# RWKV scan and attention on one core: attention's pieces joined in every third step, the inversion's products on four 64x64 tiles

## Chip, cores and metric

One NeuronCore of a Trainium2 chip runs the whole program. The metric is the device time in microseconds of one execution; a run's number is that of the core, and the number compared is the median of the runs.

## The reference

Two transformer blocks on x of 1024 x 1024, float32. The change lies in the first one, which joins an attention branch (MLA) and an RWKV-7 branch in two directions. What matters of it:

```python
# attention, 8 heads, blocks of 128 queries, 1024 keys
s = einsum('bqhd,bkhd->bhqk', qn_b, k_nope) + einsum('bqhd,bkd->bhqk', qr_b, k_rope)
p = softmax(s * scale); o = einsum('bhqk,bkhd->bqhd', p, v)

# RWKV, 8 heads of 64, one scan forward and one backward over 1024 tokens
def step(state, inp):
    r_t, w_t, k_t, v_t, a_t, b_t = inp
    sa = einsum('bhvk,bhk->bhv', state, a_t)
    state = state * w_t[:, :, None, :] + sa[..., None] * b_t[:, :, None, :] + v_t[..., None] * k_t[:, :, None, :]
    return state, einsum('bhvk,bhk->bhv', state, r_t)
```

The kernel computes the scan in tiles of 128 tokens. Within a tile the feedback through a and b is a strictly triangular matrix N for each head, and the kernel needs the inverse of I - N. With a block D of N that is 16 wide the inverse is the product (I + D)(I + D^2)(I + D^4)(I + D^8); blocks of 16 are then put together to 32, 64 and 128.

## The kernel before

**Stages.** The program of each engine is a Python function that issues its instructions in order: PE (`tensor_program`), DVE (`vector_program`), ACT (`scalar_program`), POOL and SP (loads and stores). The stages follow each other: norm and projections, MLA, shift and preparation, then `scans` (536 to about 1340 us), after it the output projections, the FFN and the second block. The change touches `scans` alone.

**The order in `scans`.** Three generators run on each engine: scan 0 (forward), scan 1 (backward) and attention. `interleave` takes one step of each in turn, to the next `yield`, and does so in the same way on every engine; I call that a round. Scan 0 gets seven rounds' start. So each queue holds: a step of scan 0, a step of scan 1, a piece of attention, and so on. An engine takes its queue strictly in order, and waits on semaphores.

**A scan.** 8 tiles, each of 2 steps of transposes (T) and 2 x 13 steps for two halves of 4 heads (u = 0, 1): An (the products that give N), D2, D4, D8, X4 (the powers of D and the partial products X of the inverse), H1 and X5 (blocks of 16 to 32), H2 and T64 (to 64), V and Y, B (to 128), U (the solved feedback), O and S (output and state). `kinds` issues the masked products M behind D2 and D8. PE writes to PSUM, DVE and ACT bring the result to SBUF, where the next step reads it. In all that is 1 + 8 x 28 = 225 steps a scan, and 232 rounds.

**Products.** `diag` multiplies 4 heads x 2 halves of the partitions with tiles (0, 0) and (64, 64) of the array. `cross` sends two of the heads to the other half of the output's partitions, so that all four 64x64 tiles are used; as two rows of tiles must not write the same bank, its results lie in a pair of banks. D4 and D8 use `cross` already. One matmul of f32 gives two records in the trace.

**PSUM.** `take` gives out the 8 banks as a ring, in the order in which PE asks; with n=2 it starts at an even bank. PE waits there for those who read the bank's last content.

**Attention.** `att_steps` yields after each part: scores of head tile i (2 matmuls of 512 columns), the 8 transposes of the probabilities of i - 1, and after every second one the product with v. That is 1 + 64 + 64 + 32 = 161 pieces. DVE takes the maximum of the scores over 1024 keys and negates it (L1127 to L1135), ACT the exp (L1148), DVE the reciprocal of the sum and the scaling (L1120 to L1125, issued ahead of the next maximum), PE transposes (L358), ACT copies.

Lines that appear in the trace: L354 and L355 matmuls, L358 transposes, L361 ACT copies, L364 DVE and POOL elementwise operations, L375 DVE's maximum, L368 DVE's scaling and negation, L1148 exp, L1280 the store of a tile's output (scan 0 from EX, scan 1 from W). Scan 0 has its buffers in AR and EX, scan 1 in X, AR and W; HT and W1 belong to attention, CS holds constants.

## Time and profile before

| | us |
|---|---|
| median of 3 runs | 3516.8 (3514.44 to 3517.77) |
| profiled execution | 3505.72 |
| its span, first to last instruction | 3503.9 |
| scan stage with attention | 536 to 1181 |
| scan stage without | 1181 to about 1340 |

Over the whole span PE is busy 96%, DVE 49%, ACT 32%, POOL 9%, and the granted clock of PE is 0.991 of full speed on average, 0.95 to 1.00 in each 100 us. A busy PE is not a PE at its peak: a small matmul is drawn with a length of its own (0.22 us), whatever the distance to the next one. Idle time on an engine costs only where another one waits for it; the chain of waits says which.

### The profile page before, as it was taken

Reading aid. Unit: us, or ns where it says so; the run is one execution under the profiler, and the core shown is the slowest. Engines: PE = TensorE matmul, PEld = TensorE weight load, DVE = VectorE, ACT = ScalarE, POOL = GpSimd, SP = SyncE. Lnnn points to the kernel's source line nnn. Section 1 sums busy time; section 2 is a strip of 40 time slices with the busy share of each in tenths; the row PEclk is TensorE's granted clock in tenths of the full one; section 3 lists DMA queues with packets and bytes.
Section 4 is the critical chain, followed back from the end, with each engine's and each line's share of the span. In section 5 each row is a group of like instructions: output and inputs, shape, how many; then the busy total and the mean of one; then the engine's idle time right before and its main releaser. Section 6 shows DMA issues by size and latency. Waiting matters only on the chain.

```text
span 3503.9 us, 61009 instructions
## 1 busy us (share of the span) xinstructions
PE 3366.8 (96%) x27176; PEld 2664.1 (76%) x27176; DVE 1713.8 (49%) x2537; ACT 1112.9 (32%) x1799; POOL 322.6 (9%) x342
## 2 busy tenths in 40 slices
PE   8989998999999999999999999999999999999998
PEld 7678776777766785587888888787778788888877
DVE  5353564665666666654345434642554522352236
ACT  4323424444444331132124212432333311241124
POOL 1131241111111222000000000001000000000000
PEclk9999999999999999999999999999999999999999
DMA  3241253111210304421112211332003111121113
GB/s 143 67 149 43 72 189 107 59 38 41 71 59 31 113 21 151 144 84 49 49 48 96 73 48 48 108 104 98 25 31 120 63 51 49 61 96 55 49 67 107
DMA packets 89973, 269.84 MB, mean 77 GB/s; under 512 B 11552, under 2 KB 12080, under 8 KB 89712
## 3 DMA queue, kind: packets, MB, share of 16 engines
q1 hardware_dynamic: 78960, 230.29, 19.9%
q0 software_dynamic: 10752, 35.66, 3.0%
q8 instruction: 214, 3.51, 0.4%
q14 instruction: 47, 0.39, 0.0%
HBM read 219.77 MB, written 46.14 MB: 76 GB/s over the span
## 4 chain that ended last, share of the span: by engine, by line
PE 82%; DVE 10%; ACT 4%; issue 2%; DMA 1%; POOL 0%; SPq 0%; DVEq 0%; ACTq 0%; POOLq 0%
PE ps L355 77%; PE ps L354 3%; DVE SM L375 2%; PE ps L358 2%; DVE AR L364 2%; ACT HT L1148 1%; DVE X L364 1%; DVE HT L368 1%; DVE W L364 1%; ACT AR L361 1%; ACT WS L361 0%; DVE WS L364 0%; DVE EX L364 0%; ACT W L2074 0%; DMA qk_d<-AR 0%
## 5 line engine op out<-in xcount | busy, mean ns | idle before, releaser
L355 PE MATMUL ps<-HH,WS 128*128 128x512 f32 (+1 forms) x3232 | 997.6, 390 | 0.0
L355 PEld LDWEIGHTS ps<-HH,WS 128*128 128x128 f32 (+1 forms) x3232 | 605.2, 187 | 128.9
L355 PE MATMUL ps<-HL,WS 128*128 128x512 f32 x1616 | 637.7, 395 | 6.3 <-DVE HL L364 5.9
L364 DVE TENSOR_TENSOR WS<-W,WS 128x1024 fp32r<-128x1024 f32 x244 | 300.2, 1230 | 617.8 <-ACT WS L361 617.8
L361 ACT ACTIVATE WS<-W 128x1024 fp32r<-128x1024 f32 x244 | 256.6, 1051 | 843.4 <-PE ps L355 836.7
L355 PE MATMUL ps<-WS,SA 128*128 128x512 f32 x2112 | 486.7, 392 | 13.6 <-DVE SA L364 11.0
L355 PEld LDWEIGHTS ps<-WS,SA 128*128 128x128 f32 x2112 | 397.4, 189 | 101.1 <-issue 15.2
L355 PEld LDWEIGHTS ps<-HL,WS 128*128 128x128 f32 x1616 | 302.6, 187 | 71.6 <-issue 6.8
L355 PE MATMUL ps<-AR 64*64 64x64 f32 (+2 forms) x5440 | 200.1, 240 | 17.2 <-ACT AR L361 9.6
L364 DVE TENSOR_TENSOR SA<-HA,SA 128x512 fp32r<-128x512 f32 x176 | 121.5, 692 | 187.3 <-ACT SA L361 187.3
L355 PE MATMUL ps<-HL,HI 128*128 128x512 f32 (+1 forms) x512 | 208.1, 406 | 3.6 <-POOL WL L364 2.8
L355 PE MATMUL ps<-WS,HL 128*128 128x512 f32 x576 | 206.4, 392 | 0.8 <-DVE X L364 0.8
L355 PE MATMUL ps<-WS,HH 128*128 128x512 f32 x640 | 202.9, 393 | 3.6 <-issue 1.5
L355 PEld LDWEIGHTS ps<-AR 64*64 64x64 f32 (+1 forms) x5440 | 154.0, 135 | 68.0 <-issue 38.2
L355 PE MATMUL ps<-HH,HI 128*128 128x512 f32 (+1 forms) x512 | 205.3, 401 | 0.0
L355 PE MATMUL ps<-HH,WL 128*128 128x512 f32 (+1 forms) x512 | 204.7, 400 | 0.0
L361 ACT ACTIVATE SA<-HA 128x512 fp32r<-128x512 f32 x176 | 110.6, 631 | 282.2 <-PE ps L355 253.5
L355 PE MATMUL ps<-HT 96*128 96x512 f32 (+1 forms) x384 | 185.7, 617 | 0.3
L361 ACT ACTIVATE AR<-ps 128x512 f32<-128x512 f32 (+4 forms) x240 | 122.2, 522 | 120.4 <-PE ps L355 83.7
L364 DVE TENSOR_TENSOR HA<-HA,ps 128x512 f32<-128x512 f32 x88 | 60.4, 687 | 184.9 <-PE ps L355 184.1
L355 PEld LDWEIGHTS ps<-WS,HH 128*128 128x128 f32 x640 | 120.2, 188 | 29.7 <-issue 1.9
L364 DVE TENSOR_TENSOR AR<-ps,CS 128x512 f32<-128x512 f32 (+1 forms) x160 | 87.4, 580 | 111.9 <-ACT AR L361 45.3
(286 smaller groups left out, 4354.1 us busy)
## 6 DMA issues: line engine op xcount, KB each, us to landing
W<-in_w_fd SPq DMA_DIRECT2D x88, 512.0 KB, 3.4
AR<-rw_d SPq DMA_DIRECT2D x104, 256.0 KB, 4.1
W<-in_w_fg SPq DMA_DIRECT2D x44, 512.0 KB, 3.4
W<-in_w_fu SPq DMA_DIRECT2D x44, 512.0 KB, 3.4
W<-in_w_tok SPq DMA_DIRECT2D x24, 512.0 KB, 3.5
rw_d<-X POOLq DMA_DIRECT2D x40, 256.0 KB, 3.4
X<-in_x SPq DMA_DIRECT2D x16, 512.0 KB, 8.9
W<-in_w_g SPq DMA_DIRECT2D x16, 512.0 KB, 3.7
```

The source lines that it names most:

```text
L354: return pe.e.matmul(o, l, r, start=start, stop=stop, skip_group_check=True)
L355: return pe.e.matmul(o, l, r, start=start, stop=stop)
L358: return pe.e.transpose(o, i, ident)
L361: return e.e.activation(o, x, ACT.Copy)
L364: return e.e.tensor_tensor(o, x, y, op)
L368: return e.e.tensor_scalar(o, x, s1, None, o1)
L375: return e.e.tensor_reduce(o, x, AX.X, op)
L1148: ae.e.activation(APB[i % 2], ps[:, b:b + 2, :].rearrange("p a b -> p (a b)"), ACT.Exp, bias=sm(264 + i % 4, 1), scale=SCALE, accum_out=sm ...
```

## The change

- `att_steps` yields once for each head tile, after scores, transposes and (every second time) the product with v: 67 pieces. On ACT the transposes' copies come ahead of exp. `one_of_three` lets attention have every third round; in the seven first rounds it has every second one.
- D2, X4, H1 and X5 use `cross` and a pair of banks each. `cross` packs its results in 128 columns of each bank of the pair. An gets 4 matmuls more, which give a turned copy of two heads' blocks.
- Sums are made ahead of the product: with DI = D^k + I the product of DI and X is X + D^k X, so X is copied from PSUM by ACT and not added by DVE. DVE adds the unit matrix to the powers (`and_one`) after ACT's copy from the same banks. H1 and X5 do the same with G1 and X1.
- POOL's sum XA is made in two parts.
- The state product of O and O's products with v move behind the next `yield`, behind U.
- The table Z64 of zeros is no longer needed.

```diff
-        def att_steps(scores, transp, pv, load):
+        def att_steps(scores, transp, pv, load, copies_first=False):
             load(0)
             yield
             for i in range(66):
                 if i % 8 == 4 and i // 8 + 1 < 8:
                     load(i // 8 + 1)
-                if i < 64:
+                if i < 64 and not copies_first:
                     scores(i)
-                    yield
                 if 1 <= i <= 64:
                     transp(i - 1)
-                    yield
+                if i < 64 and copies_first:
+                    scores(i)
                 if i % 2 and i >= 3:
                     pv((i - 3) // 2)
-                    yield
+                yield
         def skip(*_):
...
-            return att_steps(scores, transp, pv, skip)
+            return att_steps(scores, transp, pv, skip, copies_first=True)
...
-            c.DX, c.XA = pair(2), heads(256)
-            c.plus = CS[:, len(CONST) * P:len(CONST) * P + P].rearrange("p (a n) -> p a n", a=2)
+            c.DI, c.XA, c.XB = [heads(256) for _ in range(3)]
+            c.eye = cst["I64"].unsqueeze(1).broadcast_to([P, 4, 64])
...
-                            x = mm(pe, ps[o, b + h // 2, 256 * m + c0:256 * m + c0 + 64], lhs[ROWS[z], h, :], rhs[ROWS[z], h, :],
+                            x = mm(pe, ps[o, b + h // 2, c0 + 64 * m:c0 + 64 * m + 64], lhs[ROWS[z], h, :], rhs[ROWS[z], h, :],
...
-                        for n in range(2):
-                            for js in ROWS:
+                        for n in range(2 + q):
+                            for z, js in enumerate(ROWS):
                                 for j, rows in enumerate(ROWS):
                                     at_, bt = c.ART[rows, p, 0, js], c.BT[rows, p, js]
-                                    x = mm(pe, ps[js, b + j, 128 * n + 64 * q:128 * n + 64 * q + 64], bt if n else at_,
+                                    c0 = 256 if n == 2 else 128 * n + 64 * q
+                                    x = mm(pe, ps[ROWS[1 - z] if n == 2 else js, b + j, c0:c0 + 64], bt if n else at_,
                                            at_ if n else bt, True, True)
                     x.then_inc(*pe.sig(PEs, "An", i, u))
                     yield
-                    b = take(pe, PEs, "D2", i, u)
+                    b = take(pe, PEs, "D2", i, u, n=2)
                     pe.wait_ge(*at(VEs, "D1", i, u, 1))
-                    diag(b, 0, c.D1[:, 1], c.D1[:, 0])
-                    diag(b, 256, c.D1[:, 0], c.D1[:, 1]).then_inc(*pe.sig(PEs, "D2", i, u))
+                    cross(b, 0, c.D1[:, 1], c.D1[:, 0])
+                    cross(b, 128, c.D1[:, 0], c.D1[:, 1]).then_inc(*pe.sig(PEs, "D2", i, u))
                     pe.wait_ge(*at(AEs, "T", i, 3))
                     kinds(i, u, 0)
                     yield
...
-                    cross(b, 64, c.DX[:, 0], c.XA).then_inc(*pe.sig(PEs, "D4", i, u))
+                    cross(b, 256, c.DI, c.XA).then_inc(*pe.sig(PEs, "D4", i, u))
                     yield
                     b = take(pe, PEs, "D8", i, u, n=2)
                     pe.wait_ge(*at(AEs, "D4", i, u))
                     cross(b, 0, c.D4[:, 1], c.D4[:, 0])
                     pe.wait_ge(*at(VEs, "D4", i, u))
-                    cross(b, 64, c.DX[:, 0], c.DX[:, 1]).then_inc(*pe.sig(PEs, "D8", i, u))
+                    cross(b, 128, c.DI, c.XB).then_inc(*pe.sig(PEs, "D8", i, u))
                     kinds(i, u, 1)
                     yield
-                    b = take(pe, PEs, "X4", i, u)
-                    pe.wait_ge(*at(AEs, "D8", i, u))
-                    diag(b, 0, c.DX[:, 0], c.DX[:, 1]).then_inc(*pe.sig(PEs, "X4", i, u))
-                    yield
-                    b = take(pe, PEs, "H1", i, u)
-                    pe.wait_ge(*at(VEs, "X4", i, u))
+                    b = take(pe, PEs, "X4", i, u, n=2)
+                    pe.wait_ge(*at(AEs, "X3", i, u))
+                    pe.wait_ge(*at(VEs, "D8", i, u))
+                    cross(b, 0, c.DI, c.XA).then_inc(*pe.sig(PEs, "X4", i, u))
+                    yield
+                    b = take(pe, PEs, "H1", i, u, n=2)
+                    pe.wait_ge(*at(AEs, "X4", i, u))
+                    cross(b, 0, c.X1[:, 1], c.eye)
                     pe.wait_ge(*at(GEs, "G2", i, u))
-                    for h in range(4):
-                        for js in ROWS:
-                            mm(pe, ps[js, b, 64 * h:64 * h + 64], c.X1[js, 1, h, :], ident[js, js], True, True)
-                    diag(b, 256, c.G1, c.X1[:, 1]).then_inc(*pe.sig(PEs, "H1", i, u))
-                    yield
-                    b = take(pe, PEs, "X5", i, u)
+                    cross(b, 128, c.G1, c.X1[:, 1]).then_inc(*pe.sig(PEs, "H1", i, u))
+                    yield
+                    b = take(pe, PEs, "X5", i, u, n=2)
                     pe.wait_ge(*at(AEs, "H1", i, u))
-                    diag(b, 0, c.X1[:, 2], c.X1[:, 0])
-                    diag(b, 256, c.X1[:, 0], c.X1[:, 2]).then_inc(*pe.sig(PEs, "X5", i, u))
+                    pe.wait_ge(*at(VEs, "H1", i, u))
+                    cross(b, 0, c.X1[:, 2], c.X1[:, 0])
+                    cross(b, 128, c.X1[:, 0], c.X1[:, 2]).then_inc(*pe.sig(PEs, "X5", i, u))
                     yield
                     b = take(pe, PEs, "H2", i, u)
-                    pe.wait_ge(*at(VEs, "X5", i, u))
+                    pe.wait_ge(*at(AEs, "X5", i, u))
                     diag(b, 0, c.G2, c.X2[:, 1]).then_inc(*pe.sig(PEs, "H2", i, u))
...
-                    bo = take(pe, PEs, "O", i, u, n=2)
-                    state(pe, c, bo, u, 1)
                     b = take(pe, PEs, "U", i, u)
                     pe.wait_ge(*at(AEs, "Y", i, u))
                     pe.wait_ge(*at(VEs, "B", i, u))
@@ -1432,11 +1438,12 @@
                         for js in ROWS:
                             x = mm(pe, ps[js, b, 64 * h:64 * h + 64], c.TT[:, h, js], c.Y[:, h, :], True, True)
                     x.then_inc(*pe.sig(PEs, "U", i, u))
-                    b = bo
+                    yield
+                    b = take(pe, PEs, "O", i, u, n=2)
+                    state(pe, c, b, u, 1)
                     for h in range(4):
                         cc = (4 * u + h) * 64
                         rows_by(pe, b, h, c.M4[:, h, 3, :], v_[:, cc:cc + 64], False)
-                    yield
...
+            def and_one(nm, i, u, o, c0):
+                ve.wait_ge(*at(PEs, nm, i, u))
+                ve.wait_ge(*at(AEs, {"D4": "X2", "D8": "X3"}.get(nm, nm), i, u))
+                tt(ve, in_pairs(o), heads_of(bank(PEs, nm, i, u), c0), cst["I64"].unsqueeze(1).unsqueeze(1).broadcast_to([P, 2, 2, 64]),
+                   ALU.add).then_inc(*done(nm, i, u))
...
+                    tt(ve, c.XA[:, 2:4, :], ps[:, b:b + 2, 256:320], c.dT.unsqueeze(1).broadcast_to([P, 2, 64]),
+                       ALU.mult).then_inc(*ve.sig(VEs, "D1", i, u, 2))
+                    yield
+                    and_one("D2", i, u, c.DI, 0)
                     masked(i, u, 0)
                     yield
-                    ve.wait_ge(*at(AEs, "D4", i, u))
-                    tt(ve, c.DX, crossed(bank(PEs, "D4", i, u))[:, 0:2], c.plus.unsqueeze(2).broadcast_to([P, 2, 4, 64]),
-                       ALU.add).then_inc(*done("D4", i, u))
-                    yield
+                    and_one("D4", i, u, c.DI, 0)
+                    yield
+                    and_one("D8", i, u, c.DI, 0)
                     masked(i, u, 1)
                     yield
-                    ve.wait_ge(*at(PEs, "X4", i, u))
-                    ve.wait_ge(*at(AEs, "D8", i, u))
-                    tt(ve, c.X1[:, 1], hv(bank(PEs, "X4", i, u), 256), c.DX[:, 1], ALU.add).then_inc(*done("X4", i, u))
-                    yield
-                    yield
-                    ve.wait_ge(*at(PEs, "X5", i, u))
-                    tt(ve, c.X2, two(bank(PEs, "X5", i, u)), c.X1[:, 0:2], ALU.add).then_inc(*done("X5", i, u))
+                    yield
+                    and_one("H1", i, u, c.X1[:, 2], 128)
+                    yield
...
+            def both(o, nm, i, u):
+                ae.wait_ge(*at(PEs, nm, i, u))
+                cp(ae, o.rearrange("p a (g m) n -> p g a (m n)", g=2),
+                   crossed(bank(PEs, nm, i, u), 0, 256).rearrange("p g (a k) -> p g a k", a=2)).then_inc(
+                    *ae.sig(AEs, nm, i, u, frees=(PEs, nm, i, u)))
+            def one(o, nm, of, c0, i, u):
+                ae.wait_ge(*at(PEs, of, i, u))
+                cp(ae, in_pairs(o), heads_of(bank(PEs, of, i, u), c0)).then_inc(
+                    *ae.sig(AEs, nm, i, u, frees=(PEs, of, i, u)))
...
-                    copy(c.D2, two(bank(PEs, "D2", i, u)), "D2", i, u)
+                    both(c.D2, "D2", i, u)
                     yield
                     if i:
                         ae.wait_ge(*at(VEs, "vr", i - 1))
-                    copy(c.D4, crossed(bank(PEs, "D4", i, u))[:, 0:3:2], "D4", i, u)
-                    yield
-                    copy(c.DX, crossed(bank(PEs, "D8", i, u))[:, 0:2], "D8", i, u)
-                    yield
-                    yield
-                    copy(c.X1[:, 0::2], two(bank(PEs, "H1", i, u)), "H1", i, u)
-                    yield
+                    both(c.D4, "D4", i, u)
+                    one(c.XB, "X2", "D4", 256, i, u)
+                    yield
+                    one(c.XA, "X3", "D8", 128, i, u)
+                    yield
+                    copy(in_pairs(c.X1[:, 1]), heads_of(bank(PEs, "X4", i, u), 0), "X4", i, u)
+                    yield
+                    one(c.X1[:, 0], "H1", "H1", 0, i, u)
+                    yield
+                    both(c.X2, "X5", i, u)
+                    ae.also(AEs, "X5", i, u)
...
-                    tt(ge, c.XA, c.D1[:, 1], bc(cst["I64"], 4), ALU.add).then_inc(*ge.sig(GEs, "X", i, u))
+                    ge.wait_ge(*at(VEs, "D1", i, u, 2))
+                    for g, src_ in enumerate((c.D1[:, 1, 0:2, :], c.XA[:, 2:4, :])):
+                        x = tt(ge, c.XA[:, 2 * g:2 * g + 2, :], src_, bc(cst["I64"], 2), ALU.add)
+                    x.then_inc(*ge.sig(GEs, "X", i, u))
                     ge.wait_ge(*at(AEs, "An", i, u))
...
-            for _ in range(7):
+            for n in range(7):
                 next(s0)
-                next(at_)
-            interleave(s0, s1, at_)
+                if n % 2 == 0:
+                    next(at_)
+            interleave(s0, s1, one_of_three(at_))
             e.close("scans", e.name)
+        def one_of_three(gen):
+            for _ in gen:
+                yield
+                yield
+                yield
         def nothing():
```

## Rows read from the trace of the kernel before

**Rows 1.** The stretches of the stage: busy time of each engine, clock, DMA.
```profile
core 0: us, PE busy (x) PEld busy (x) DVE busy (x) ACT busy (x) POOL busy (x), PEclk, DMA share, GB/s
536.00:1181.00 645.00, 593.42 (x11465) 450.46 (x11465) 387.27 (x716) 277.38 (x572) 101.21 (x120) 0.99 0.18 54
1181.00:1340.00 159.00, 146.54 (x4198) 128.58 (x4193) 100.10 (x196) 55.79 (x118) 35.44 (x42) 1.00 0.20 66
```

**Rows 2.** Timeline of SP: stores of scan 0's tiles (start, length, queue, line).
```profile
767.26 0.34 SPq L1280 DMA_DIRECT2D o_d<-EX  x1
880.62 0.34 SPq L1280 DMA_DIRECT2D o_d<-EX  x1
989.18 0.34 SPq L1280 DMA_DIRECT2D o_d<-EX  x1
...
1204.13 0.32 SPq L1280 DMA_DIRECT2D o_d<-EX  x1
...
1267.35 0.32 SPq L1280 DMA_DIRECT2D o_d<-EX  x1
```

**Rows 3.** The chain of waits by line, 536 to 1181 and 1181 to 1340 us.
```profile
by line: PE ps L355 43.5%; DVE SM L375 9.8%; ACT HT L1148 6.9%; PE ps L358 6.9%; PE ps L354 6.3%; DVE HT L368 4.9%; issue 3.6%; DVE AR L364 3.0%; DVE X L364 2.1%; DVE W L364 2.0%; ACT AR L361 1.9%; DVE EX L364 1.6%; DVE SM L368 1.6%; ACT X 
...
by line: PE ps L355 51.2%; PE ps L354 17.4%; DVE AR L364 4.4%; issue 3.6%; ACT AR L361 3.4%; DVE W L364 3.1%; DVE SM L375 2.7%; DVE EX L364 2.5%; ACT X L361 1.5%; PE ps L358 1.5%; DVE X L364 0.9%; DVE AR L1519 0.9%; DVE X L1519 0.9%; DVE W 
```

**Rows 4.** Waits, 536 to 1181 us: total, times, longest.
```profile
ACT HT L1148 <- DVE SM L368: 214.9, 64, 5.3
```

**Rows 5.** Timeline of PE: sets X5 and H2 (two tiles), An (four).
```profile
1248.62 1.15 PE L355 MATMUL ps<-AR 64*64 64x64 f32 x32
...
1267.97 0.68 PE L355 MATMUL ps<-W,AR 64*64 64x64 f32 x16 [0.37 <-DVE W L364]
...
1268.66 0.69 PE L355 MATMUL ps<-AR 64*64 64x64 f32 x32
```

**Rows 6.** Timeline: reading 512, 256 and 128 columns on ACT and DVE.
```profile
1245.69 0.42 DVE L364 TENSOR_TENSOR AR<-ps,AR 128x256 f32<-128x256 f32 x1 [0.63 <-PE ps L355]
...
1247.41 0.60 ACT L361 ACTIVATE AR<-ps 128x512 f32<-128x512 f32 x1 [1.94 <-PE ps L355]
...
1249.81 0.69 DVE L364 TENSOR_TENSOR EX<-ps,AR 128x512 f32<-128x512 f32 x1 [3.23 <-PE ps L355]
...
1250.89 0.29 DVE L364 TENSOR_TENSOR W<-ps,W 128x128 f32<-128x128 f32 x1 [0.39 <-PE ps L354]
...
1251.50 0.38 ACT L361 ACTIVATE AR<-ps 128x256 f32<-128x256 f32 x1 [0.61 <-PE ps L355]
...
1252.84 0.73 POOL L364 TENSOR_TENSOR AR<-X,CS 128x256 f32<-128x256 f32 x1 [13.30 <-DVE X L364]
```

**Rows 7.** Timeline of attention's own instructions: product with v, scores, softmax, transposes.
```profile
911.42 0.27 PE L355 MATMUL ps<-EX,HT 128*64 128x128 f32 x1
...
911.53 0.27 PE L355 MATMUL ps<-EX,HT 128*64 128x128 f32 x1
...
913.58 1.98 PE L355 MATMUL ps<-HT 96*128 96x512 f32 x4
...
915.50 0.62 PE L355 MATMUL ps<-EX,AR 64*64 64x64 f32 x7
...
915.76 1.21 DVE L375 TENSOR_REDUCE SM<-ps 128x1 f32<-128x1024 f32 x1
...
917.20 1.11 ACT L1148 ACTIVATE HT<-ps,SM 128x1024 f32<-128x1024 f32 x1 [2.29 <-DVE SM L368]
918.21 0.19 ACT L1148 ACTIVATION_READ_ACCUMULATOR HT<-ps,SM 128x1 f32 x1
...
923.08 0.15 DVE L1123 RECIPROCAL SM<-SM 128x1 f32<-128x1 f32 x1
923.27 0.75 DVE L368 TENSOR_SCALAR HT<-HT,SM 128x1024 f32<-128x1024 f32 x1
```

**Rows 8.** Timeline of PE and its weight loads: from 64x64 tiles to transposes and back.
```profile
904.06 0.68 PE L355 MATMUL ps<-CS,AR 64*64 64x64 f32 x16
904.58 0.63 PE L355 MATMUL ps<-AR 64*64 64x64 f32 x16
905.14 1.09 PE L358 MATMUL ps<-CS,X 128*128 128x128 f32 x8
905.14 0.86 PEld L358 LDWEIGHTS ps<-CS,X 128*128 128x128 f32 x8
...
912.50 0.54 PEld L355 LDWEIGHTS ps<-EX,AR 64*64 64x64 f32 x15 [0.17 <-issue]
```

**Rows 9.** Timeline: DVE's product beside POOL's, and the same one alone.
```profile
902.32 2.54 POOL L364 TENSOR_TENSOR X<-AR,X 128x512 f32<-128x512 f32 x2 [14.00 <-PE ps L354]
902.50 1.22 DVE L364 TENSOR_TENSOR W<-W,SM 128x128 f32<-128x128 f32 x1
...
1251.22 0.29 DVE L364 TENSOR_TENSOR W<-W,SM 128x128 f32<-128x128 f32 x1
```

19 lines of the change are left out of this document (10 added, 9 removed).

## The prediction

> **What bounds the kernel now.** The table of stretches comes first [rows 1]. The change touches only the scan stage, from 536 to about 1340 us. It has two parts: up to 1181 us attention runs beside the two scans, after that the scans are alone. TensorE (PE) is busy 593.42 of 645 us and 146.54 of 159 us. That hides what is lost, because each small matmul is drawn as at least 0.22 us long however closely the next one follows, so I count starts.
>
> The second view is the stores of `o_d` [rows 2]. One tile of one scan, 28 steps, takes 113.4 and 108.6 us beside attention and 63.2 us (1204.13 to 1267.35) without it, that is 2.25 us for a round of two steps. The attention part has 161 pieces of attention, one for each round: 645/161 = 4.0 us per round. So attention costs 645 - 161 x 2.25 = 283 us, 4.4 us for each of its 64 head tiles.
>
> The third is the chain of waits, once for either part [rows 3]. Beside attention PE holds some 57% of the chain; the maximum on VectorE (DVE) has 9.8%, the exp on ScalarE (ACT) 6.9%, the scaling of the probabilities 4.9%: it is the latency of attention between the engines, on queues that the scans need too. ACT stands idle for 214.9 us in front of its 64 exps, waiting for the negated maximum [rows 4], and the scans' copies stand queued behind it. Alone, the scans have PE on 70% of the chain.
>
> PE's idle time is at least 645 - 593 = 52 and 159 - 147 = 12 us [rows 1]. Counted by starts (each start minus what the record ahead of it needs, over all records of the stage) I put its waits at 106 us beside attention and 27 us after, an estimate: 0.66 us for each of 161 rounds and 0.38 for each of 71.
>
> **Part 1, the sets of the inversion on four tiles.** In `diag` a set uses two of the four 64x64 tiles of the array, in `cross` all four. One 64x64 f32 matmul leaves two records. X5, 32 records on two tiles, is drawn 1.15 us long, H2 with 16 records 0.68 us; An, 32 records on four tiles, 0.69 us [rows 5]. The last record's own 0.22 us taken off: (1.15 - 0.22)/31 = 30 ns a record on two tiles, (0.69 - 0.22)/31 = 15 ns on four. The change turns D2 (32 records), X4 (16), H1 (32) and X5 (32) into `cross`: 112 records x 15 ns = 1.7 us by these; for whole sets, whose four-tile forms keep about 0.49 us for 32 records up to the next set (32 x 15 ns), against 0.88 to 0.92 us now, it is 0.39 + 0.19 + 0.41 + 0.43 = 1.42 us, which I take. There are 32 such passes (2 scans, 8 tiles, 2 halves): -45 us. An gets 4 matmuls more, 8 x 15 ns x 32 = +4 us. PE's work falls by about 41 us.
>
> What of it stays depends on the way from a set to the next of the same scan. PE's end to a reader's start takes some 0.1 us, with the end drawn 0.2 us after the last start; ACT needs 0.60 us for 512 columns and 0.38 for 256, DVE 0.69 and 0.42 [rows 6]. From the last start to the next set:
> - D4 to D8: ACT copies 512 (0.60), then 256 more, then DVE adds the unit matrix on 256 (0.42), for 0.60 + 0.69 in before: +0.1 us.
> - D8 to X4: 0.38 and then 0.42 in place of 0.60: 1.2 for 0.95 us, most of it hidden by the masked products (M) that PE issues behind D8.
> - X4 to H1: a copy of 0.38 for a sum of 0.42: 0.73 for 0.77 us.
> - H1 to X5: 0.38 then 0.42, one behind the other, for 0.60: 1.2 for 0.95 us.
> - X5 to H2: 0.60 for 0.69: 0.95 for 1.04 us.
>
> A wait shows where the other scan's step is shorter than this way. Scan 0 is seven steps ahead, so H1 of one stands beside U of the other once a tile. U's step falls from 1.15 us (48 records: the state product of O, U, and O's products with v) to 0.44 us (its own 16 on two tiles' pace), as these move behind the next yield, where they cover the wait for ACT's copy of U instead. H1's way of 1.2 us, covered before, then shows 0.75 us. An to D2 (1.1 us) beside X5, now 0.49 for 0.93 us, shows 0.44 more; the two ways to X5 beside An and beside the transposes show 0.4, the ones to D8 0.2. Together 1.8 us a tile, 14 us over 8 tiles. Part 1: -41 + 14 = -27 us. Ends: -41 (nothing given back) and 0 (all of it).
>
> ACT gets some 0.9 us more a pass (0.6 x 2 + 0.38 x 4 + 0.6 for 0.6 x 4) and DVE 0.25 us less; neither is full beside attention, 277 and 387 of 645 us [rows 1]. Were the copies to set the pace all the same, nothing of the 41 us would stay: the second rival. The page TensorEngine Tiling (Array Packing) of the Trainium skill, section PSUM Bottleneck, speaks for that rival: packing speeds up TensorE and not the evacuation of PSUM, so that copies may become the limit after it.
>
> Hidden at nothing: DVE's third product after An (a 128x128 operation took 0.29 us [rows 6]) stands behind D2's inputs, with ACT's copy of An and GpSimd's (POOL) sum queued behind it; the first is read five steps on at H1, the second at D4, a step and M later. If POOL is late, D4's third set waits: at most its 0.73 us, now in two instructions. Sets in pairs of banks: D2, X4, H1 and X5 take two banks, 28 for 24 a pass, of 8 in a ring. A bank comes round again after about two rounds, by when it was read; after a joined piece it can still be the scores' (below). I take +4 us, ends 0 and +15.
>
> **Part 2, the pieces of attention joined.** A head tile of attention is 4 records of scores, which hold PE 1.92 us (913.58 to 915.50), 8 transposes at 0.107 us, and half of 32 records at 0.054 us for the product with v: 1.92 - 0.2 + 0.86 + 0.87 = 3.45 us [rows 7, 8]. Going from one shape of tile to another costs extra: the transposes at 905.14 start 0.15 us after the last start of H1's 64x64 records (904.58 + 0.63 - 0.22 = 904.99), inside H1 the same step between equal shapes is 0.06, and the weight loads show 0.17 us of issue there [rows 8]. So 0.09 us for a change. Before, a head tile has 5 such changes (in and out of scores, of transposes, and half the time of the product), after it has 2.5: -0.23 us, 14 us over 64. What is left of the 4.4 us are waits, about 0.5 us a head tile (4.4 - 3.45 - 0.45).
>
> After, in a joined piece that begins when scan 1's step is issued (T): scores until T + 1.9. The transposes need DVE's scaling of the tile before, which is queued behind DVE's work for both scans (about T + 1.4 on average) and takes 0.15 + 0.75 us: T + 2.4, so PE waits 0.5 to 0.6 us. Then DVE takes the maximum (1.21), ACT the two copies of the transposes and exp (1.11 + 0.19), from T + 4.2 to T + 5.4. Scan 0's next step leaves PE at T + 4.1, or 1.75 us later where the product with v follows, and its copy on ACT stands behind exp; PE wants it at T + 4.9 and gets it at T + 6.0. That is 0.7 to 1.1 us every second time, about 0.4 on average. The piece hides the 0.38 us which a round loses anyway. Sum: 0.6 + 0.4 - 0.4 = 0.6 us for 0.5. So 3.45 + 0.23 + 0.6 = 4.25 to 4.3 for 4.4 us: -0.15 x 64 = -10 us. The ends: no wait shows and the piece still covers a round (3.3 us: -70 us), or both come in full each time, 1.1 us for exp and 1.3 for a DVE slowed by POOL as the product at 902.50 was (1.22 for 0.29 us beside POOL's products [rows 9]): 2.0 us of waits for 0.5 after the 0.4 hidden, 5.7 us a piece, +80 us.
>
> Moved with it: SP's loads of the next head are issued every eighth head tile, 24 rounds apart for 20, far ahead of use; the first loads of the output projection come 36 rounds before the end instead of 71, still about 80 us. On SP only two stores of `o_d` a scan stand behind them, since the last tile's inputs went out by round 178 and attention ends in round 196 of 232.
>
> **The sum.** -27 + 4 - 10 = -33, and some 3 us for O's products that now stand ahead of the wait for U: -36 us. The profiled execution took 3505.7 us (span 3503.9); the three runs have a median of 3516.8, 11 us more, and I carry the difference over: 3516.8 - 36 = 3481 us.
>
> **The rivals.**
> - The joined pieces free both scans. For it: 22% of the chain beside attention is maximum, exp and scaling, and two rounds of three are free of them. Against it: ACT still has the exp in order, ahead of the scans' copies. With the 0.6 us gone it is -50 for -10: about 3440 us. Chance 0.2.
> - PE's saving all comes back as waits, copies setting the pace: 3516.8 + 4 - 10 - 3 = 3508 us, near no change. Against it: alone, PE has 70% of the chain. Chance 0.14.
> - Slower: PE's queue stands in the joined piece for the scaling, then again for ACT behind exp, since X4 and X5 are now ACT's too. Break-even is 36/64 = 0.56 us more per piece than I took (1.2 in all for 0.6). With exp's 1.1 us in every piece and 0.8 for the scaling it is 1.5: 3.45 + 0.23 + 1.5 = 5.2 for 4.4 us, +50, so 3516.8 - 27 + 4 - 3 + 50 = 3541 us. For it: 214.9 us of ACT's idle time before exp. Chance 0.16.
> - The forecast, 3481 us (its own range 3455 to 3506): 0.5.
>
> A measurement can tell about 0.2%, 7 us. Faster by more: 0.5 + 0.2, and 0.02 of the second, 0.72. Within: 0.11. Slower: 0.17. The range of 8 in 10 takes in the first rival's near half and the better half of the slow one: 3430 to 3530.
>
> **What would show it.** Starts of X5's 32 records in about 0.7 us; the scan alone at 59 to 60 us a tile for 63.2, and beside attention 3.5 us a round (196 rounds in some 690 us) for 4.0; the stage from 536 to about 1305 us; ACT's idle time before exp well under 214.9 us; the transposes' wait on PE for the scaling at 0.6 us. It is wrong if a tile alone stays at 63 us, if PE waits over 1.2 us in a joined piece, or if the time outside 536 to 1340 moves.

## The result, and the profile after

The changed kernel takes 3522.6 us (median of 20 runs, 3515.2 to 3528.4), the kernel before 3516.5 us (20 runs, 3507.8 to 3520.9). The ratio is 1.0019, with a 95% interval of 1.0012 to 1.0026: 6 us or 0.2% slower, for a forecast of 36 us faster. The profiled execution of after took 3515.2 us, with a span of 3513.4; it lies 7 us under its median, that of before 11 us under its own, so the two traces are 9.5 us apart where the medians are 6.

The stretches of after, in the columns of [rows 1]: attention beside the scans up to 1256 us (1181 before), then the scans alone.
```profile
core 0: us, PE busy (x) PEld busy (x) DVE busy (x) ACT busy (x) POOL busy (x), PEclk, DMA share, GB/s
535.00:1256.00 721.00, 629.99 (x13767) 477.03 (x13765) 423.26 (x838) 332.80 (x713) 123.97 (x169) 0.99 0.18 54
1256.00:1341.00 85.00, 72.57 (x2142) 61.64 (x2141) 48.19 (x102) 31.51 (x73) 18.29 (x25) 0.95 0.23 77
```
PE is busy for 703 us in the stage, against 740 in [rows 1]: PE's work went away, the time did not. ACT has 364 us for 333, DVE 471 for 487.

The stores of scan 0's tiles, SP's timeline as in [rows 2], and the last one of scan 1:
```profile
647.28 0.34 SPq L1287 DMA_DIRECT2D o_d<-EX  x1
...
1167.21 0.34 SPq L1287 DMA_DIRECT2D o_d<-EX  x1
...
1266.73 0.32 SPq L1287 DMA_DIRECT2D o_d<-EX  x1
...
1329.20 0.32 SPq L1287 DMA_DIRECT2D o_d<-EX  x1
1343.15 0.32 SPq L1287 DMA_DIRECT2D o_d<-W  x1
```
and the last one in the kernel before:
```profile
1340.49 0.32 SPq L1280 DMA_DIRECT2D o_d<-W  x1
```
From SP's first load for attention (535.37 us after, 536.60 before) to this store the stage takes 808 us, for 804 before. So it is no shorter, and of the 9.5 us between the two traces only 4 lie in it.

Beside attention a tile takes (1167.21 - 647.28)/5 = 104.0 us. Attention now lasts 196 rounds in 720 us, 3.67 us a round (4.0 before, 3.5 forecast). A tile of the scans alone takes 62.5 us, for 63.2 in [rows 2] and a forecast of 59 to 60. So both parts of the change fell short.

The chain of waits by line, first beside attention, then alone, as in [rows 3]:
```profile
by line: PE ps L355 34.5%; PE ps L354 10.3%; PE ps L358 8.5%; DVE AR L364 6.9%; DVE HT L368 6.0%; issue 4.2%; ACT W L361 4.0%; ACT AR L361 3.9%; ACT HT L1148 3.7%; DVE X L364 3.6%; DVE W L364 2.2%; DVE SM L375 1.9%; DVE EX L364 1.7%; ACT X 
...
by line: PE ps L355 41.3%; PE ps L354 21.3%; DVE AR L364 7.3%; issue 7.2%; ACT AR L361 5.7%; DVE EX L364 2.1%; DVE SM L375 2.0%; DVE W L364 1.7%; ACT X L361 1.4%; POOL AR L364 1.2%; DVE W L1577 1.0%; DVE X L364 0.8%; ACT X L1617 0.7%; ACT A
```
DVE's maximum falls from 9.8 to 1.9% and the exp from 6.9 to 3.7%, as hoped. In their place stand the scans' reads of PSUM: DVE on AR 6.9% for 3.0, ACT on AR 3.9% for 1.9; alone, 7.3 and 5.7% for 4.4 and 3.4. The scaling (DVE HT) is at 6.0% for 4.9.

The waits beside attention: engine and line that wait, whom for, total us, times, longest. First the kernel before, rows that [rows 4] doesn't have:
```profile
DVE AR L364 <- ACT AR L361: 38.6, 23, 3.0
...
PE ps L355 <- ACT AR L361: 11.8, 11, 2.0
...
PE ps L355 <- DVE AR L364: 2.5, 8, 0.5
...
PE ps L358 <- DVE HT L368: 1.9, 2, 1.0
```
and after:
```profile
DVE AR L364 <- ACT AR L361: 135.3, 78, 5.1
ACT W L361 <- PE ps L358: 124.2, 47, 4.8
...
PE ps L358 <- DVE HT L368: 42.5, 46, 2.5
...
PE ps L355 <- DVE AR L364: 24.5, 36, 1.8
...
PE ps L355 <- ACT AR L361: 3.6, 3, 1.6
...
ACT HT L1148 <- DVE SM L368: 2.6, 1, 2.6
```
Two waits on PE have grown. Its transposes (L358) wait for DVE's scaling of the probabilities, 46 times and 42.5 us for 1.9. That is more than the growth: before, the view puts most of the transposes' waits down to other releasers, and counted by starts (below) they are 48 us for 22. Its sets (L355) wait for DVE's sum of the unit matrix, 24.5 us for 2.5, and less for ACT's copies, 3.6 us for 11.8: together 28.1 for 14.3. The sum in turn waits 135.3 us for ACT's copy out of the same banks, on an idle DVE. ACT's 214.9 us ahead of exp [rows 4] are 2.6 now, but only since the copies of the transposes, which now stand ahead of it in ACT's queue, do the waiting (124.2 us).

### The profile page after: what moved, and what is told of

The parts are those of the page before. It is cut to its first block, busy times and chain, and to the rows that moved or that the text cites. A ratio compares the mean times of both kernels' runs of the same rounds, so it can differ in the third digit from the quotient of the medians.

```text
span 3513.4 us, 61758 instructions
## 1 busy us (share of the span) xinstructions
PE 3333.9 (95%) x27432; PEld 2627.5 (75%) x27432; DVE 1701.3 (48%) x2569; ACT 1143.8 (33%) x1895; POOL 328.0 (9%) x374
## 4 chain that ended last, share of the span: by engine, by line
PE 80%; DVE 10%; ACT 5%; issue 2%; DMA 1%; POOL 1%; SPq 0%; DVEq 0%; ACTq 0%; POOLq 0%
PE ps L355 74%; PE ps L354 3%; PE ps L358 3%; DVE AR L364 2%; DVE X L364 1%; DVE HT L368 1%; ACT AR L361 1%; ACT W L361 1%; DVE SM L375 1%; ACT HT L1148 1%; DVE W L364 1%; DVE WS L364 1%; ACT WS L361 0%; POOL AR L364 0%; ACT W L2109 0%
## 5 line engine op out<-in xcount | busy, mean ns | idle before, releaser
L355 PE MATMUL ps<-HH,WS 128*128 128x512 f32 (+1 forms) x3232 | 1001.0, 391 | 0.0
L355 PEld LDWEIGHTS ps<-HH,WS 128*128 128x128 f32 (+1 forms) x3232 | 607.1, 188 | 129.1
L355 PE MATMUL ps<-HL,WS 128*128 128x512 f32 x1616 | 640.1, 396 | 9.7 <-DVE HL L364 5.9
L355 PE MATMUL ps<-WS,SA 128*128 128x512 f32 x2112 | 485.2, 391 | 15.0 <-DVE SA L364 12.5
L355 PEld LDWEIGHTS ps<-WS,SA 128*128 128x128 f32 x2112 | 396.4, 188 | 102.1 <-issue 14.7
L355 PEld LDWEIGHTS ps<-HL,WS 128*128 128x128 f32 x1616 | 303.4, 188 | 75.5 <-issue 6.8
L355 PE MATMUL ps<-HL,HI 128*128 128x512 f32 (+1 forms) x512 | 207.8, 406 | 3.2 <-POOL WL L364 2.8
L355 PE MATMUL ps<-WS,HL 128*128 128x512 f32 x576 | 206.5, 392 | 0.8 <-DVE X L364 0.8
L355 PE MATMUL ps<-WS,HH 128*128 128x512 f32 x640 | 203.0, 393 | 3.6 <-issue 1.5
L355 PE MATMUL ps<-AR 64*64 64x64 f32 (+2 forms) x5568 | 168.4, 241 | 39.7 <-DVE AR L364 29.7
L355 PE MATMUL ps<-HH,WL 128*128 128x512 f32 (+1 forms) x512 | 204.8, 400 | 0.0
L355 PE MATMUL ps<-HH,HI 128*128 128x512 f32 (+1 forms) x512 | 204.5, 399 | 0.0
L364 DVE TENSOR_TENSOR AR<-ps,CS 128x256 f32<-128x256 f32 (+2 forms) x256 | 111.6, 469 | 163.3 <-ACT AR L361 152.8
L361 ACT ACTIVATE AR<-ps 128x256 f32<-128x256 f32 (+4 forms) x304 | 132.5, 447 | 160.4 <-PE ps L355 96.5
L355 PE MATMUL ps<-HT 96*128 96x512 f32 (+1 forms) x384 | 182.7, 609 | 1.8 <-ACT X L1621 1.4
L355 PEld LDWEIGHTS ps<-AR 64*64 64x64 f32 (+1 forms) x5568 | 120.8, 135 | 75.1 <-issue 32.2
L361 ACT ACTIVATE W<-ps 128x512 f32<-128x512 f32 (+2 forms) x228 | 114.1, 533 | 177.7 <-PE ps L358 124.2
```

What stands on the lines that cost most here:

```text
L355: return pe.e.matmul(o, l, r, start=start, stop=stop)
L361: return e.e.activation(o, x, ACT.Copy)
L364: return e.e.tensor_tensor(o, x, y, op)
```

## Experiments

All ratios are to the kernel before on the same chip, with 95% intervals; 0.1% is 3.5 us. "Waits in the stage" are PE's idle times counted by starts from the one profiled execution, as in the prediction, but with the need of each shape of record more finely set: the kernel before has 114 us of waits by it (the prediction had 133) and 688 of work, the changed one 163 and 643. The expectations give letters to theories: A, the inversion keeps its gain, and B, the saved work comes back as waits; C, O's early banks are in the way; D, O's products were a cover; E, the 28 banks cost; F, the joined piece waits for the scaling; G, the loss is the longer ways and the banks, and the pace is worth little; H, the pace brings its 41 us and copies, sums and banks eat it; K, the earlier scaling is the whole gain; L, joining has one of its own.

| run | inversion | O | attention | median, us | ratio |
|---|---|---|---|---|---|
| changed kernel | new | moved | joined | 3522.6 | 1.0019 [1.0012, 1.0026] |
| e1 | new | - | separate | 3544.9 | 1.0083 [1.0066, 1.0099] |
| e2 | old | moved | joined | 3525.5 | 1.0028 [1.0017, 1.0038] |
| e5 | old | moved | separate | 3511.5 | 0.9984 [0.9976, 0.9993] |
| e6 | old, pairs of banks | moved | separate | 3519.3 | 1.0017 [1.0007, 1.0026] |
| e7 | new | moved | separate | 3518.9 | 1.0015 [1.0005, 1.0025] |
| e8 | new | moved | joined, scaling earlier | 3491.3 | 0.9930 [0.9917, 0.9944] |
| e9 | old | moved | joined, scaling earlier | 3490.7 | 0.9926 [0.9914, 0.9939] |
| e10 | new, other order | moved | joined | 3524.9 | 1.0027 [1.0016, 1.0037] |
| e11 | new, two sums left out | moved | joined | 3504.7 | 0.9957 [0.9943, 0.9971] |
| e12 | new, sets on two tiles | moved | joined | 3547.8 | 1.0094 [1.0078, 1.0110] |
| e13 | old | moved | separate, scaling earlier | 3496.4 | 0.9942 [0.9930, 0.9955] |
| e14 | new | moved | separate, scaling earlier | 3492.9 | 0.9928 [0.9915, 0.9942] |

### Which part: e1 and e2

e1 takes the changed kernel's inversion alone. e2 takes the joined pieces and O's products behind U. There is no run of the joined pieces without that move: by the order of the program O's two banks would be held while a joined piece asks for banks of the same ring, and PE would wait for what it frees only later (argued). e1's core, in the changed kernel:
```
-                    yield
+                    bo = take(pe, PEs, "O", i, u, n=2)
+                    state(pe, c, bo, u, 1)
                     b = take(pe, PEs, "U", i, u)
```


> Only the inversion part of the change (D2, X4, H1, X5 on four tiles, unit matrix added to the powers); attention's pieces and O's products stay as in the kernel before. Theory A (the inversion keeps its gain, the joining of attention loses more): about 25 us faster than before, 3490 us. Theory B (the saved PE time comes back as waits for the copies wherever it is): within 7 us of before.

> Attention's pieces joined in every third step and O's products behind U, the inversion as before. Theory A: slower than before by 20 to 30 us, with some 50 us of waits in front of the transposes, as in the changed kernel. Theory B: within 7 us of before.

Measured: +0.83% and +0.28%, 28 and 9 us over the kernel before of the same batch; neither theory had e1 slower by so much, and e2 lies between the two. Each part by itself is slower than the kernel before, and together they are less slow than either. In e1 PE's work in the stage falls to 649 us as forecast, but its waits rise from 114 to 189 us, 31 of them at one place, the first products of a tile (S), where there were none before: with 28 banks a pass, O's pair, taken early, meets the ring (argued from the order in which banks are taken; what was measured is that e7, with O moved, has about 1 us of waits at S and is 0.68% faster than e1). So the new inversion needs O moved, and the parts can't be added up from these two runs alone. In e2 the transposes' waits are 34 us for 22. The mean granted clock over e1's runs is 0.982 for 0.988.

### Without attention: e3 and e4

All of attention ahead of the scans, in the kernel before (e3) and in the changed one (e4):
```
+            for _ in at_:
+                pass
             for n in range(7):
                 next(s0)
-                next(at_)
-            interleave(s0, s1, at_)
+            interleave(s0, s1)
```


> The kernel before with all of attention issued ahead of the two scans, so that the trace shows each alone. The scans alone should take 225 rounds x 2.2 us = about 500 us, attention alone 64 head tiles at over 4 us, since nothing hides its maximum, exp and scaling.

> The changed kernel with all of attention ahead of the scans. Theory A: the scans alone take 25 to 30 us less than in e3. Theory B: the scans alone take the same as in e3 to 5 us, although PE's records fall by 41 us.

A single run each: 3556.6 and 3569.9 us. The waits of the scans alone, e3 first, then e4:
```profile
DVE AR L364 <- ACT AR L361: 28.4, 31, 3.5
...
PE ps L355 <- DVE AR L364: 6.8, 25, 1.0
```
```profile
DVE AR L364 <- ACT AR L361: 116.1, 82, 4.0
...
PE ps L355 <- DVE AR L364: 36.4, 62, 1.8
```
The stretches of the scans, e3 first:
```profile
857.00:1390.00 533.00, 493.50 (x13859) 431.57 (x13860) 339.83 (x654) 191.50 (x400) 123.99 (x144) 0.97 0.17 55
853.00:1393.00 540.00, 463.42 (x14114) 388.79 (x14115) 323.82 (x686) 217.04 (x496) 128.54 (x176) 0.96 0.17 55
```
Attention is the same in both (286 us each). From their first to their last product the scans alone take 531 us in e3 and 538 in e4. Counted by starts, work goes from 450 to 409 us, the 41 us of the prediction, and waits from 81 to 129. That is theory B, and 2 us more than its margin of 5. The waits grew at X4 (6.6 to 19.5 us), X5 (5 to 16), An (2.5 to 11) and D2 (4 to 11). So the loss of the inversion's gain does not need attention. A place of it, the timeline of e4:
```profile
1001.88 0.63 ACT L1617 ACTIVATE X<-X 128x512 f32<-128x512 f32 x1 [1.74 <-DVE X L364]
...
1002.42 0.58 ACT L1618 ACTIVATE X<-ps 128x512 f32<-128x512 f32 x1
1002.89 0.59 ACT L1621 ACTIVATE X<-ps 128x512 f32<-128x512 f32 x1
1003.37 0.39 ACT L361 ACTIVATE AR<-ps 128x256 f32<-128x256 f32 x1
1003.63 0.40 ACT L361 ACTIVATE W<-ps 128x256 f32<-128x256 f32 x1
1003.86 1.62 DVE L364 TENSOR_TENSOR AR<-ps,CS 128x256 f32<-128x256 f32 x3 [2.01 <-ACT AR L361]
...
1004.43 0.46 PE L355 MATMUL ps<-AR 64*64 64x64 f32 x16 [1.61 <-DVE AR L364]
```
ACT is held by three exps of the other scan and then copies XA (1003.37); only then may DVE, idle for 2.01 us, add the unit matrix (1003.86), and PE's 16 records of X4 wait 1.61 us. Most of this wait is ACT's queue, in which the copy stood before the change too; the sum behind it is what the change adds. X4's records took two tiles and 0.46 us before; on four tiles they start within 0.24 us.

### O and the banks: e5, e6, e7

e5 moves O behind U in the kernel before and changes nothing else. e6 adds pairs of banks for the four sets, the second left unused. e7 is the changed kernel with attention in separate pieces.
```
-                    b = take(pe, PEs, "X4", i, u)
+                    b = take(pe, PEs, "X4", i, u, n=2)
```


> The kernel before with one edit: O's state product and O's products with v behind U, as in the change. Theory C (the two banks of O, held over the other scan's step and the piece of attention, are what PE waits for once the sets take more banks): no change by itself, within 7 us, as the kernel before shows no waits at S. Theory D (the products are good cover for ACT's copy of U): 5 to 10 us faster.

> The kernel before with O moved as in e5 and D2, X4, H1 and X5 taking two banks each, the second left unused; their products are the old ones. It is the price of the banks alone. Theory C: with O moved it costs little, under 7 us against e5. Theory E (28 banks a pass for 24 make PE wait wherever the ring comes round, and that ate the 41 us of PE's work): 15 us or more slower than e5.

> The change without the joining of attention: inversion on four tiles and O moved. e1, which lacked the move of O, had 31 us of waits in front of S and took 28 us more than before. Theory C: those 31 us go, so about 3516 us, equal to before within 7 us. Theory E: still 15 us or more over before.

O's move is worth 0.16%, 5.6 us (interval 2 to 8), which both theories C and D allow. The pairs of banks cost 1.0017 - 0.9984 = 0.33%, 11.6 us, without a single instruction changed (the two intervals together leave 7 to 16). That lies between theory C's 7 us and theory E's 15. e7's waits at S are gone and it lies within 7 us of before, as theory C had it. The whole new inversion on top of O costs 1.0015 - 0.9984 = 0.31%, 11 us. So apart from its banks it brings nothing and costs nothing, within 5 us, for all of its 41 us of PE work. By the starts e7 has 40 us less of PE's work in the stage than e6 and 38 us more of waits.

### What the four tiles bring: e10 and e12

e10 tries to take the pace away by issuing the heads in the order 0, 1, 2, 3, so that two tiles are used in a row. e12 has the four sets on the two tiles of the diagonal as before, all else as changed:
```
-                            o = ROWS[1 - z if h > 1 else z]
+                            o = ROWS[1 - z if h > 1 and turned else z]
```
(`turned` is False for D2, X4, H1 and X5.)

> The changed kernel with the products of D2, X4, H1 and X5 issued head by head, so that only two tiles work at a time; data, banks, copies and sums are those of the changed kernel. PE's records of these sets go back to about 30 ns, 45 us of work in all. Theory G: the four-tile pace is worth little, since the next set waits for ACT and DVE anyway: 5 to 15 us over the changed kernel. Theory H (the four tiles bring their 41 us, and copies, sums and banks cost as much): 35 us or more over it, about 3560 us.

> The changed kernel, with the sets D2, X4, H1 and X5 on the two tiles of the diagonal, where they were before the change (heads 2 and 3 are not turned to the other half of the output, so what these sets put together is wrong and the output is not the reference's). Everything else of the change stays: the bank pairs, the sums of unit matrices, the third product for XA, the copies, O moved, the joined pieces. From the first to the last start a D2 set took 0.88 us on two tiles and 0.48 on four, X4 0.46 and 0.24, H1 and X5 0.93 and 0.48; with 32 half tiles of each that is 32 x (0.40 + 0.22 + 0.45 + 0.45) = 49 us of TensorE's work that this run gives back. Theory G (TensorE's pace in these sets is worth little since the way through ACT and DVE is what each scan waits for, and the other scan and attention fill in): 5 to 15 us over the changed kernel of this batch, ratio to the kernel before 1.003 to 1.006, and the idle time of TensorE in the stage falls from 163 to about 125 us. Theory H (the four tiles bring their whole saving and the added copies, sums and banks eat it): 35 us or more over the changed kernel, ratio 1.011 or more, and the idle time stays at 155 us or more.

e10 doesn't take the pace away: from first to last start X5 took 0.52 us for 0.48. With all four tiles in use the order in which they are served hardly matters, and the run says nothing on what the pace is worth. In e12 X5's sets are as before the change:
```profile
1296.89 1.15 PE L355 MATMUL ps<-AR 64*64 64x64 f32 x32
```
against this set of the changed kernel:
```profile
1283.71 0.69 PE L355 MATMUL ps<-AR 64*64 64x64 f32 x32
```
PE's work in the stage is 690 us (643 changed), its waits 148 (163), and the kernel is 25 us slower than the changed one (3547.8 for 3522.6). That is between the two theories, which had 5 to 15 and 35 us, and waits of 125 and 155: of 49 us of PE work in these sets about half is worth time, the other half comes back as waits of a PE that is ready before its inputs are. So in the changed kernel the four tiles gain 25 us (the two intervals together leave 20 to 32), and as the whole new inversion gains nothing (e7), the rest of it gives them back.

### The sums one behind the other: e11

The changed kernel without DVE's sums at D8 and at H1, PE reading ACT's copy in place of them at H1 and an older sum at D8:
```
-                    and_one("D8", i, u, c.DI, 0)
...
-                    and_one("H1", i, u, c.X1[:, 2], 128)
```


> The changed kernel without the sums of the unit matrix at D8 and H1: it leaves them out, and X4 and X5 read older sums, so that they wait for ACT's copy alone. It prices the second operation in a row from PSUM. Theory G: X4's and X5's waits on PE, 12.2 and 14.2 us in the changed kernel, fall to under half and the time by 10 us or more. Theory B (queues of ACT decide, not the second operation): within 5 us of the changed kernel.

3504.7 us, 0.62% under the changed kernel by the ratios, 18 us by the medians. Its waits beside attention:
```profile
DVE AR L364 <- ACT AR L361: 81.7, 35, 6.0
...
PE ps L358 <- DVE HT L368: 33.2, 41, 2.2
...
PE ps L355 <- ACT AR L361: 11.7, 12, 1.6
PE ps L355 <- DVE AR L364: 8.2, 21, 1.2
```
PE's wait for the sum falls from 24.5 to 8.2 us, but 8 us of that now stand as a wait for ACT's copy, 11.7 for 3.6. Counted by starts the waits at X5 fall from 14 to 5.5 us, those at X4 by some 5 of 12, short of the half that theory G wanted; its 10 us or more of time came. A second reader of the same banks, which starts when ACT's copy is done, at two of the four places in a pass that have one, so costs at most 18 to 22 us. At most, because the run does two things more: it takes 64 additions off DVE, which helps attention (its transposes wait 39 us for 48), and banks come free without the second reader. These were not told apart.

A rough account of the new inversion on top of O: -25 us for the pace, +11.6 for the banks, up to +18 to 22 for these two sums, up to +4 for An's added products (the prediction's figure). That makes 5 to 13 us, and e7 against e5 is +11. The pace and the sums were measured in the joined kernel, so this shows that the terms are of the right size, and no more.

### The joined piece and its scaling: e8, e9, e13, e14

In the changed kernel DVE scales the probabilities of tile i - 1 in the same piece in which PE wants to transpose them. e8 and e9 put the scaling of tile i on DVE one turn of the scans behind its maximum, two turns ahead of the piece that transposes it; e9 has the old inversion.
```
             def scores(i):
-                if i:
-                    scale(i - 1)
                 ve.wait_ge(*at("pe_att", "sc", i))
...
+            def steps():
+                for n, _ in enumerate(att_steps(scores, skip, skip, skip)):
+                    yield
+                    later(n - 1)
+                    yield
```
(`later(i)` is `scale(i)`.)

> The changed kernel with one edit: DVE scales the probabilities of a head tile one round ahead of the piece that transposes them, two rounds after their exp, and not in front of the next maximum. Theory F (PE's 48 us in front of the transposes are the wait for DVE's scaling in the same piece): the wait falls by 25 us or more and the time by 15 to 25 us against the changed kernel, about 3500 us. Against it: DVE's 0.9 us then stands in front of a scan's step and shows there; the time stays within 7 us of 3522.

> Joined pieces, O moved and the scaling a round earlier as in e8, with the inversion of the kernel before (two tiles, one bank, sums in DVE). Against e8 it gives the inversion's worth where attention no longer holds PE. Theory G (the inversion's saved PE time is lost to longer ways from set to set and to banks in any arrangement): within 7 us of e8's 3491 us, or below it. Theory A: 20 us or more above e8.

3491.3 and 3490.7 us, 0.70 and 0.74% faster than the kernel before: 31 us under the changed kernel, where theory F had 15 to 25, and 35 under e2. The attention part of e8, waits:
```profile
PE ps L358 <- DVE HT L368: 1.1, 3, 0.4
```
42.5 us are 1.1 now. The place to see it is the timeline of the changed kernel, then of e8, each with scores, scaling and transposes of a piece:
```profile
899.74 1.98 PE L355 MATMUL ps<-HT 96*128 96x512 f32 x4
899.86 1.29 DVE L364 TENSOR_TENSOR X<-ps,CS 128x512 f32<-128x512 f32 x2
...
901.07 0.15 DVE L1123 RECIPROCAL SM<-SM 128x1 f32<-128x1 f32 x1
901.26 0.75 DVE L368 TENSOR_SCALAR HT<-HT,SM 128x1024 f32<-128x1024 f32 x1
901.93 1.22 DVE L375 TENSOR_REDUCE SM<-ps 128x1 f32<-128x1024 f32 x1
...
902.16 1.07 PE L358 MATMUL ps<-CS,HT 128*128 128x128 f32 x8 [0.43 <-DVE HT L368]
```
```profile
893.21 0.99 DVE L368 TENSOR_SCALAR HT<-HT,SM 128x1024 f32<-128x1024 f32 x1
...
897.55 1.98 PE L355 MATMUL ps<-HT 96*128 96x512 f32 x4
...
899.37 1.04 PE L358 MATMUL ps<-CS,HT 128*128 128x128 f32 x8
...
899.57 1.23 DVE L375 TENSOR_REDUCE SM<-ps 128x1 f32<-128x1024 f32 x1 [1.09 <-PE ps L355]
```
The transposes follow the scores without a gap, though the scaling is slower here (0.99 us, POOL at work beside it).

Whether joining the pieces has a part in that was still open. e13 and e14 leave attention in separate pieces and move the scaling alone, e13 with the old inversion, e14 with the new:
```
             def scores(i):
-                if i:
-                    scale(i - 1)
+                if i == 1:
+                    scale(0)
...
             def transp(i):
-                if i == 63:
-                    scale(i)
+                if i < 63:
+                    scale(i + 1)
```


> The kernel before with O moved, its attention in separate pieces as before, and VectorE's scaling of tile i put in its piece after the maximum of tile i instead of ahead of the maximum of tile i+1, so one turn of the scans earlier. The same kernel without the earlier scaling was 0.9984 of the kernel before, the joined pieces with the earlier scaling 0.9926. In the kernel before the transposes cost TensorE 22 us of waiting in the stage. Theory K (the earlier scaling is the whole gain of the joined kernels, and joining has none of its own): the transposes' wait falls to 3 us or less and the ratio is 0.990 to 0.9945, at 3482 to 3497 us. Theory L (joining has its 10 us or more of its own from fewer changes of mode and fewer, longer stretches): the ratio stays at 0.995 or above, at 3499 us or more.

> The same on the changed kernel's inversion: attention in separate pieces, O moved, scaling a turn earlier. Without the earlier scaling this was 1.0015 of the kernel before; the joined kernel with the earlier scaling 0.993. Theory K (joining has nothing of its own): 0.991 to 0.9955, within 0.3% of the joined kernel with the earlier scaling. Theory L (joining brings 10 us or more): 0.9965 or above. Between this run and e13 stands what the new inversion is worth where the transposes no longer wait: in the joined kernels it was 0.0004 of the time, no difference; a new inversion that pays once attention is out of the way would be 0.003 or more below e13.

0.9942 and 0.9928. e14 lies 0.02% from the joined kernel on the same inversion, e13 0.16% above, with overlapping intervals. So the earlier scaling is the gain (15 us on e5, 26 on e7, by the medians), as theory K had it. Joining has 0 to 6 us of its own by the middle values; the intervals don't exclude 12. The transposes' wait is 8 and 13 us, not the 3 that was expected. Under early scaling the new inversion is worth 0.14% in separate pieces and -0.04% in joined ones: no difference that these runs can tell.

## Why the prediction was wrong

By ratios of the runs, in us (3516 x the difference), the steps from before to after are: O -5.6, pairs of banks +11.6, the rest of the new inversion -0.7 (e7 against e6), joined pieces +1.4; sum +6.7. The forecast had -3, +4, -27, -10. The measured time lies inside the stated range of 3430 to 3530 us, but the range reached that far only to take in part of the slow rival; the sum of the forecast, 3481 us, is 42 us off, and the two terms that carry it both failed.

- **PE's work in the inversion** was right: -41 us in e3 against e4, X5's records drawn in 0.69 us.
- **What of it stays** failed: +14 us of waits forecast, 48 measured in e4 against e3. The step that failed is "a wait shows where the other scan's step is shorter than this way", worked out at a few pairs of steps. Where it looked closely it was near: at X5 it had 0.75 and 0.4 us a tile, 9 us over 8 tiles, for 11 measured. The rest came where it had put nothing or little. The way from D8 to X4 was "most of it hidden by the masked products", and X4's waits grew by 13 us; An had no term and grew by 8.5; D2 had 3.5 us for 7. The ways themselves were sized about right: 0.25 us longer at D8 and at H1, and e11 gives at most 0.3 us back for each of 64 sums. So it is the share of them that is covered that was too high: all of PE's saving comes back in e4, and half of the pace's in e12. That shorter sets cover less of each other's ways is argued from An and D2, whose own ways the change leaves about as they were; no run isolated it. The second rival (all of PE's saving comes back as waits) had this part right, given 0.14. The rule of the Trainium skill, page TensorEngine Tiling (Array Packing), section PSUM Bottleneck, that after packing the evacuation of PSUM may be the limit, agrees with these runs in direction: 25 us gained by the pace in e12, about as much given back by reads and banks. But it is the latency of the reads and not their amount: ACT is busy 364 and DVE 471 us of some 806.
- **The banks**: +4 us forecast, 11.6 measured, inside its ends of 0 and +15. "By when it was read" was argued from averages; e6 shows that four more banks a pass cost time with no instruction changed. By the counts of e5 and e6 the waits of the stage rise by 7 us, 3.0 at H1, 2.7 at S and 2.2 each at O and Y; which release they stand for was not isolated.
- **The joined piece** failed: -10 us forecast, +1.4 on the new inversion and 0.44% or 15.5 us on the old one (e2 against e5, which differ in the joining alone). The saving by fewer changes of tile shape was put at 14 us; by the counts PE's work falls by 4 us in e2 against e5 and by 7 in e9 against e13, so the 0.09 us for a change, read at one place, was at least twice too high. The wait for the scaling was named and sized (0.5 to 0.6 us a piece; 48 us over 64 pieces are 0.75), but then booked against the 0.5 us of waits of a head tile that go and 0.4 that the piece covers. That booking is the step that failed: in e2 the transposes' waits are some 16 us above e5's, as much as the whole loss. In the changed kernel they are 26 us above the kernel before. The third rival's mechanism (PE held in the joined piece by the scaling) was at work, at some 0.4 us a piece more than before; its second half, PE behind exp, shows as 0.38 us at single places (a set at 914.86 that waits for exp and a copy).
- **O** was right in sign, -3 for -5.6, with 2 to 8 by the interval.
- **The tests**: "wrong if a tile alone stays at 63 us": it did, at 62.5. "Wrong if PE waits over 1.2 us in a joined piece": it waited up to 2.5 us in front of the transposes. A round came to 3.67 us for 3.5, and the stage ends at 1343 us for 1305. Outside the stage the span has 2706 us for 2700, with the same instructions there; over the traces of all the runs it is 2698 to 2710, so this is a spread between executions and no work of the change.

Where a change halves a producer's time, and what reads it gets longer, the whole forecast hung on one number, the part of the saving that stays, worked out at five places of one tile. It was between 0 and 41 us by the prediction's own ends, and nothing in the trace of before excluded 0.

**A faster kernel** came of it: the changed kernel with the scaling a turn earlier (joined e8 3491 us, separate e14 3493), or the old inversion with O moved and the same scaling (joined e9 3491, separate e13 3496), 0.6 to 0.7% under the kernel before. The least edit that does most of it is O's move and four lines on DVE (e13).

## What to carry to other kernels

When engines hand work over in turns, an operation on an engine that is not full can still cost the bottleneck time by its place in the queue: move what another engine will want (here a scaling of 0.9 us, worth 15 to 35 us over 64 of them) to an earlier slot, behind the point at which its inputs are ready. Before packing matmuls tighter, count the readers that stand in a row between a set and the next, and the banks: here a second reader (at most 18 to 22 us) and four more banks a pass (11.6 us) ate the 25 us that the packing gained. A way between two sets may be called hidden only after it was looked at in every step beside which it runs: here one that was called hidden cost 13 us. Test a saving on the bottleneck engine by giving it back alone (e12) before believing its share.

## What the runs showed of the hardware

**The granted clock is lower in kernels with more short waits; the cause is not shown.** Over all runs the mean granted TensorE clock is 0.988 for the kernel before, 0.986 changed, 0.982 in e1 with its 189 us of waits, 0.987 to 0.988 with the earlier scaling. Time x clock is 3475 us for both the kernel before and the changed one: by this product, which takes all of the time as if it went with that clock, they are equal, and the 6 us go with the clock. One place, the changed kernel, in two stretches of 8 us and PE's timeline:
```profile
1152.00:1160.00 8.00, 5.38 (x72) 3.13 (x62) 4.95 (x9) 4.47 (x10) 0.00 (x0) 0.87 0.01 2
1160.00:1168.00 8.00, 7.91 (x128) 6.13 (x124) 4.87 (x10) 1.96 (x4) 2.55 (x2) 0.70 0.01 2
```
```profile
1156.47 1.06 PE L358 MATMUL ps<-CS,HT 128*128 128x128 f32 x8 [2.09 <-DVE HT L368]
```
PE stood 2.09 us for the scaling and was busy 5.38 of the first 8 us; the clock is 0.87 and 0.70 of full in the two stretches, so part of them ran at the lower of the two levels, 1.2 GHz. That the waits are the cause is read from such places and from the order of the means; no run held the waits apart from the rest. Single executions differ by as much: e5's trace has about the same waits in the stage as that of the kernel before, at a mean clock of 0.975 there for 0.992.

**The number of tiles in use, not their order, set the pace here.** 32 records of 64x64 f32 matmuls start within 0.48 us on four tiles, 0.93 on two, and 0.52 on four served two at a time (e10).
